# A streaming encoder layer in float32 on one core: the first block's order, S5 output by quarters, and other places for the later mixers

## The reference, cut to what matters

```python
h = rmsnorm(x, norm_mix); z = h @ w_in                 # 1024 x 1536: xl, gl, us of 512 each
xc, new_conv = causal_conv(xl, conv_buf, conv_w, conv_b)      # 4 taps
r, ig = sigmoid(xc @ wa + ba), sigmoid(xc @ wx + bx)          # 8 heads of 64
a = exp(-8 * r * softplus(-lam)); b = sqrt(1 - a*a) * (ig * xc)
hl = scan(h[t] = a[t]*h[t-1] + b[t]); y_lru = hl * gelu(gl)
ys = s5(us)      # 32 groups of 16 channels, 64 complex states each, diagonal recurrence
g = gelu(ys); y_ssm = g * sigmoid(g @ w_glu + b_glu)
mix = concat(rmsnorm(y_lru), rmsnorm(y_ssm)); x = x + mix @ w_out
h2 = rmsnorm(x, norm_ffn); x = x + (silu(h2 @ w_gate) * (h2 @ w_up)) @ w_down   # d_ff 2816
y = rmsnorm(x, norm_final)
```

## Time and profile before

| | us |
|---|---|
| median of 3 runs | 2478.4 (2475.61 to 3758.57) |
| profiled execution, its own time | 2483.81 |
| its span, first to last instruction | 2482.0 |
| TensorE busy | 2244.3 (90%), 11746 matmul records |
| VectorE / ScalarE / GpSimd busy | 1549.7 / 1110.4 / 408.3 |
| mean granted TensorE clock | 0.945 |

### The profile page before, as it was taken

How to read it: one execution, slowest core, us unless ns; L and a number is a source line. 1 busy time by engine, 2 the same in 40 slices (tenths; PEclk the granted TensorE clock), 3 DMA queues, 4 the chain that set the end, 5 groups by cost and what they waited for, 6 DMA issues and landing times.

```text
span 2482.0 us, 30507 instructions
## 1 busy us (share of the span) xinstructions
PE 2244.3 (90%) x11746; PEld 2173.5 (88%) x11746; DVE 1549.7 (62%) x2601; ACT 1110.4 (45%) x1481; POOL 408.3 (16%) x483
## 2 busy tenths in 40 slices
PE   4546589999999999998999999899999989999995
PEld 3536489998899999898999999899999989999995
DVE  6465454667666665876567477656667766664544
ACT  3342433465454356546344454544455544433231
POOL 2453111013110110230111024011102311010001
PEclk9775699999999999999999999999999989999998
DMA  4346133355433535453344546333555543343331
GB/s 146 105 124 176 47 121 118 125 152 164 147 101 107 171 107 154 160 164 113 112 136 154 138 130 203 94 119 110 175 140 152 145 128 111 104 145 119 110 123 52
DMA packets 191073, 322.84 MB, mean 130 GB/s; under 512 B 82896, under 2 KB 121104, under 8 KB 190800
## 3 DMA queue, kind: packets, MB, share of 16 engines
q1 hardware_dynamic: 188560, 313.54, 41.8%
q0 software_dynamic: 2368, 7.34, 1.0%
HBM read 296.39 MB, written 26.53 MB: 130 GB/s over the span
## 4 chain that ended last, share of the span: by engine, by line
PE 78%; DVE 4%; SPq 3%; ACT 2%; POOL 2%; issue 2%; DMA 1%; POOLq 0%; DVEq 0%; ACTq 0%
PE acc L787 25%; PE acc L789 24%; PE acc L788 24%; SPq L449 3%; PE acc L863 1%; PE acc L864 1%; DVE rstd L1041 1%; PE acc L873 1%; POOL tmp L511 1%; PE acc L843 1%; DVE w_hl L924 1%; PE acc L853 1%; DMA g_dram<-u 1%; DVE act_hl L924 1%; POOL s5p L536 0%
## 5 line engine op out<-in xcount | busy, mean ns | idle before, releaser
L787 PE MATMUL acc<-act_hl,w_hl 128*128 128x416 f32 x2640 | 951.8, 361 | 59.0 <-DVE act_hl L924 55.3
L789 PE MATMUL acc<-act_hl,w_hl 128*128 128x416 f32 x2640 | 940.6, 356 | 0.0
L788 PE MATMUL acc<-act_hl,w_hl 128*128 128x416 f32 x2640 | 938.1, 355 | 0.0
L924 DVE TENSOR_TENSOR w_hl<-w_raw,w_hl 128x1024 fp32r<-128x1024 f32 x440 | 545.3, 1251 | 115.0 <-ACT w_hl L611 113.4
L787 PEld LDWEIGHTS acc<-act_hl,w_hl 128*128 128x128 f32 x2640 | 507.6, 192 | 77.9 <-issue 54.6
L788 PEld LDWEIGHTS acc<-act_hl,w_hl 128*128 128x128 f32 x2640 | 507.9, 192 | 8.8 <-issue 3.1
L789 PEld LDWEIGHTS acc<-act_hl,w_hl 128*128 128x128 f32 x2640 | 506.4, 192 | 1.8
L611 ACT ACTIVATE w_hl<-w_raw 128x1024 fp32r<-128x1024 f32 x440 | 454.8, 1051 | 91.0 <-DMA w_raw<-in_w_ffn 45.7
L924 DVE TENSOR_TENSOR x_acc<-x_acc,acc 128x416 f32<-128x416 f32 x480 | 272.5, 585 | 228.6 <-PE acc L789 222.9
L511 POOL TENSOR_TENSOR tmp<-tmp 128x416 f32<-128x416 f32 x135 | 169.7, 1257 | 1193.2 <-ACT tmp L619 1184.6
L787 PE MATMUL acc<-ff_hl,w_hl 128*128 128x416 f32 x880 | 315.1, 358 | 24.8 <-DVE x_acc L924 22.0
(11 more groups left out here) (157 smaller groups left out, 1815.6 us busy)
## 6 DMA issues: line engine op xcount, KB each, us to landing
w_raw<-in_w_ffn SPq DMA_DIRECT2D x330, 512.0 KB, 3.7
w_raw<-in_w_in SPq DMA_DIRECT2D x60, 512.0 KB, 3.5
w_raw<-in_w_out SPq DMA_DIRECT2D x40, 512.0 KB, 3.3
s5y<-y_dram SPq DMA_DIRECT2D x80, 256.0 KB, 4.2
...
```

The costliest lines, as they stand in the source:

```text
L787: pe.matmul(out, w(0), x(0), start=first, stop=False)
L788: pe.matmul(out, w(0), x(1), start=False, stop=False)
L789: return pe.matmul(out, w(1), x(0), start=False, stop=last)
L924: return v.tensor_tensor(out, x, y, op)
```

## The change

1. FIRST is rewritten. The steps are smaller: tb is cut into tb (GpSimd's eight operations), ts (ScalarE's sines) and tr (GpSimd's last operation and its stores); w0 is one unit per step; pb's ScalarE part becomes pq and stands before n1; the VectorE part of xl becomes cv and that of ga becomes bx; the z store becomes zst; c1's store moves into ck. The table steps stand between the products of us, gl and xl, with gl ahead of xl. The LRU steps (la to ld, and xl, cv, ga, bx of tiles 2 and 3) stand between the steps of S5. x comes in two halves, and two units of weights ahead of the parameters.
2. c1t and bmt have two buffers each, tq0 a place of its own, zero lies in kj1 (so ck(1) waits for zero_st). The S5 token buffers begin 6656 bytes further up.
3. The S5 output goes by quarters: gst(j) stores quarter j in 8 DMAs, gld(j) loads it with one, gs(j) splits it. g_dram has another layout.
4. MIXER, the order of all later mixers, is rewritten with the same small steps. Its last step stands at place 60 instead of 64.

The diff, cut to its core:

```diff
+FIRST = [("x", 0), ("pa", 0), ("sq1", 0), ("w0", 0), ("sq1", 1), ("w0", 1), ("sq1", 2), ("w0", 2), ("sq1", 3), ("tb", 0),
+         ("pq", 0), ("n1", 0), ("h1", 0), ("h1", 1), ("h1", 2), ("h1", 3),
+         ("us", 0), ("ts", 0), ("tr", 0), ("tb", 1), ("pb", 0), ("us", 1), ("pc", 0), ("us", 2), ("c1", 0), ("us", 3),
+         ("ts", 1), ("tr", 1), ("tb", 2), ("zst", 0), ("c1", 1), ("gl", 0), ("ck", 0), ("c1", 2), ("gl", 1), ("ck", 1), ("c1", 3),
+         ("gl", 2), ("ck", 2), ("bm", 0), ("ts", 2), ("tr", 2), ("tb", 3), ("gl", 3), ("ck", 3), ("bm", 1), ("bt", 0),
+         ("xl", 0), ("bm", 2), ("bt", 1), ("kt", 0), ("cv", 0), ("bm", 3), ("bt", 2), ("xl", 1), ("ts", 3), ("tr", 3), ("bt", 3),
+         ("zl", 0), ("pl", 0), ("ga", 0), ("bx", 0), ("cv", 1), ("ga", 1), ("bx", 1), ("s5", 0), ("la", 0), ("s5", 1), ("lb", 0),
+         ("s5", 2), ("lc", 0), ("s5", 3), ("ld", 0), ("s5", 4), ("ld", 1), ("xl", 2), ("s5", 5), ("cv", 2), ("s5", 6), ("xl", 3),
+         ("ga", 2), ("s5", 7), ("bx", 2), ("cv", 3), ("gst", 0), ("s5", 8), ("ga", 3), ("bx", 3), ("s5", 9), ("la", 1), ("gld", 0),
+         ("s5", 10), ("lb", 1), ("gst", 1), ("s5", 11), ("lc", 1), ("s5", 12), ("gs", 0), ("ld", 2), ("s5", 13), ("ld", 3),
+         ("gld", 1), ("s5", 14), ("gst", 2), ("s5", 15), ("gs", 1), ("nls", 0), ("s5", 16), ("gld", 2), ("s5", 17), ("gst", 3),
+         ("nls", 1), ("nl", 0), ("gs", 2), ("gld", 3), ("ml", 0), ("ml", 1), ("gs", 3), ("glu", 0), ("glu", 1), ("ns", 0),
+         ("ms", 0), ("ms", 1)] + [("out", d) for d in range(KD)] + [("sq2", 0), ("n2", 0)] + [("h2", i) for i in range(4)]
...
-        LOW = top[0]
+        LOW = top[0] = top[0] + 6656
...
-        zero = sb("zero", [HG, GE, 7 * HG])
+        KJ1 = top[0] + GE * 8 * HG * 4
         kj = [sb(f"kj{i}", [HG, GE, 8, HG]) for i in range(2)]
-        c1t, bmt, rt = [sb(n, [P, GE, 9, HG]) for n in ("c1t", "bmt", "rt")]
-
-        tq = [at("tq0", [P, GE, W5], F32, BB3)] + [sb(f"tq{i}", [P, GE, W5]) for i in (1, 2)]
+        zero = at("zero", [HG, GE, 7 * HG], F32, KJ1)
+        c1t, bmt = [[sb(f"{n}{i}", [P, GE, 9, HG]) for i in range(2)] for n in ("c1t", "bmt")]
+        rt = sb("rt", [P, GE, 9, HG])
+
+        tq = [sb(f"tq{i}", [P, GE, W5]) for i in range(3)]
...
-            load_x(0)
+            for h in range(2):
+                sp.dma_start(x_acc[0][:, 4 * h:4 * h + 4, :], a["x"][0][:, 4 * h:4 * h + 4, 0:T]).then_inc(x_half[h], 16)
+            for u in range(2):
+                load_unit(u)
             for dst, name in ((bc[:], "bc"), (ident[:], "ident"), (dsk[:], "dsk")):
                 sp.dma_start(dst, a[name]).then_inc(par_b, 16)
             sp.dma_start(jrow[:], a["jrow"][:, 0:W5]).then_inc(par_b, 16)
             sp.dma_start(lmask[:], a["lmask"][:, 0:W5]).then_inc(par_b, 16)
-            for u in range(3):
+            for u in range(2, RING):
...
+                elif kind == "zst":
+                    for e in range(KL):
+                        wait_evacuated(sp, ("us", b, e))
                     if b >= 2:
                         sp.wait_ge(u_in, 16 * L * (b - 1))
                     sp.dma_start(z_dram[b % 2].rearrange("e g h s c -> (g h) e (s c)"),
                                  zs[:].rearrange("p e s c -> p e (s c)")).then_inc(z_st, 16)
+                elif kind == "gst":
+                    wait_evacuated(sp, ("y5", b, 4 * j + 1))
+                    wait_evacuated(sp, ("y5", b, 4 * j + 2))
+                    wait_evacuated(sp, ("y5", b, 4 * j + 3))
+                    if b >= 2:
+                        sp.wait_ge(ys_in[j], 16 * (b - 1))
+                    for s in range(L):
+                        sp.dma_start(g_dram[b % 2][j, :, :, s, :].rearrange("g h c -> h g c"),
+                                     u5[s * HG:(s + 1) * HG, j * GE:(j + 1) * GE, :]).then_inc(g_st[j], 16)
+                elif kind == "gld":
+                    sp.wait_ge(z_st, 16 * (b + 1))
+                    sp.wait_ge(g_st[j], 16 * L * (b + 1))
+                    sp.dma_start(zs[:, j].rearrange("p s c -> p (s c)"), g_dram[b % 2][j].rearrange("g h s c -> (g h) (s c)"))\
+                      .then_inc(ys_in[j], 16)
...
+                elif kind == "tr":
+                    g = slice(j * GE, (j + 1) * GE)
+                    po.wait_ge(rho_done, 1)
...
-                elif kind == "c1":
+                elif kind == "ck":
+
                     po.wait_ge(c1_done, j + 1)
-                    po.dma_start(y_dram[:, j * GE:(j + 1) * GE, 0:P], c1t[:, :, 1:9, :].rearrange("p g t h -> p g (t h)"))\
-                      .then_inc(c1_st, 16)
-                elif kind == "ck":
+                    po.dma_start(y_dram[:, j * GE:(j + 1) * GE, 0:P], c1t[j % 2][:, :, 1:9, :].rearrange("p g t h -> p g (t h)"))\
+                      .then_inc(c1_st[j % 2], 16)
...
+                    act.wait_ge(ys_in[j], 16 * (b + 1))
                     if j == 0:
-                        act.wait_ge(ys_in, 16 * G * (b + 1))
                         wait_m(act, ("xl", b, KL - 1))
-                    for n in (2 * j, 2 * j + 1):
-                        act.activation(tokens(act_hl[b % 2][:, 0, KL + n, :]), natural(zs[:, n]), ACT.Copy).then_inc(g_hi, 1)
+                        wait_m(act, ("gl", b, KL - 1))
+                    act.activation(tokens(act_hl[b % 2][:, 0, KL + j, :]), natural(zs[:, j]), ACT.Copy).then_inc(g_hi, 1)
...
+                    if j >= 2:
+                        v.wait_ge(c1_st[j % 2], 16 * (j // 2))
+                        v.wait_ge(ck_prod, 2 * (j - 1))
                     if j:
-                        v.wait_ge(c1_st, 16 * j)
-                        v.wait_ge(ck_prod, 2 * j)
+                        v.wait_ge(c1_done, j)
+                    table(j, 9, c1t[j % 2], bb[:, 2], 0, bc[:, 3], 1, 8, SUB).then_inc(c1_done, 1)
+                elif kind == "bm":
+                    if j >= 2:
+                        v.wait_ge(bt_prod, 2 * (j - 1))
+                    if j:
                         v.wait_ge(bm_done, j)
-                    table(j, 9, c1t, bb[:, 2], 0, bc[:, 3], 1, 8, SUB).then_inc(c1_done, 1)
-                elif kind == "bm":
-                    if j:
-                        v.wait_ge(bt_prod, 2 * j)
-                    v.wait_ge(c1_done, j + 1)
-                    table(j, 8, bmt, bb[:, 0], 0, bb[:, 1], 2, 0, ADD).then_inc(bm_done, 1)
+                    else:
+                        v.wait_ge(c1_done, KL)
+                    table(j, 8, bmt[j % 2], bb[:, 0], 0, bb[:, 1], 2, 0, ADD).then_inc(bm_done, 1)
...
-                elif kind == "xl":
+                elif kind == "cv":
                     if (b, j) == (0, 0):
                         v.wait_ge(par_c, 64)
                     if j >= 2:
                         v.wait_ge(ylru_done, b * KL + j - 1)
-                    wait_evacuated(v, step)
+                    wait_evacuated(v, ("xl", b, j))
...
-                elif kind == "ga":
-                    wait_evacuated(v, (*step, 1))
+                elif kind == "bx":
+                    wait_evacuated(v, ("ga", b, j, 1))
...
```

More of the change, by code:

```diff
@@ L219, in build @@
         bb = sb("bb", [P, 4, G, HG])
-        BB3 = top[0] - G * HG * 4
         pw = sb("pw", [P, 3, G, NPOW])
@@ L264, in build @@
         dt_done, ang_done, pow_done, pl_done = sem("dt_done"), sem("ang_done"), sem("pow_done"), sem("pl_done")
-        c1_done, c1_st, ck_prod, kj_free, kj_done = sem("c1_done"), sem("c1_st"), sem("ck_prod"), sem("kj_free"), sem("kj_done")
+        c1_done, ck_prod, kj_free, kj_done = sem("c1_done"), sem("ck_prod"), sem("kj_free"), sem("kj_done")
+        c1_st = [sem(f"c1_st{i}") for i in range(2)]
         k_st, zero_st, kt_st = [sem(f"k_st{i}") for i in range(2)], sem("zero_st"), sem("kt_st")
@@ L270, in build @@
         t_st, tau_done, bb_done = [sem(f"t_st{i}") for i in range(3)], sem("tau_done"), sem("bb_done")
+        x_half = [sem(f"x_half{i}") for i in range(2)]
         x_in = [sem(f"x_in{i}") for i in range(2)]
@@ L285, in build @@
         w_done, p_made, x_made, p_done = sem("w_done"), sem("p_made"), sem("x_made"), sem("p_done")
-        g_st, ys_in, g_hi, g_lo, yssm_done = sem("g_st"), sem("ys_in"), sem("g_hi"), sem("g_lo"), sem("yssm_done")
+        g_st, ys_in = [sem(f"g_st{e}") for e in range(KL)], [sem(f"ys_in{e}") for e in range(KL)]
+        g_hi, g_lo, yssm_done = sem("g_hi"), sem("g_lo"), sem("yssm_done")
         nrm, nrm_hi, nrm_lo = sem("nrm"), sem("nrm_hi"), sem("nrm_lo")
@@ L651, in _ @@
                 elif kind == "w0":
-                    for u in range(LEAD_HI):
-                        weight_hi(u)
+                    weight_hi(j)
                 elif kind == "ck":
+                    if j == 1:
+                        act.wait_ge(zero_st, 16 * KL)
                     if j >= 2:
@@ L827, in _ @@
                             ins = pe.matmul(acc[0:HG, bank, (g % 4) * P:(g % 4 + 1) * P], bb[:, 0, j * GE + g, :],
```

(17 more changed lines are left out.)

63 lines of the change are left out of this document (19 added, 44 removed), and 25 rows, old and new, of tables (FIRST, MIXER).

## The result

| | before | after | forecast |
|---|---|---|---|
| median of the runs | 2478.4 us (2475.6 to 2481.4) | 2576.2 us (2573.6 to 2582.2) | 2506 (2425 to 2552) |
| ratio, 95% interval | 1 | 1.0397 [1.0375, 1.0419] | |
| profiled execution, span | 2482.0 | 2571.8 | |
| gate(0) of block 0 starts | 346.75 | 310.26 | 291 |
| S5 of the first block starts | 195 | 154.3 | 133 |

One execution of before, at 3758.6 us, lies half as high again as the three others and is left out. The kernel is slower by 4.0%, outside the range of the forecast. The first block gained 36 us where 56 were forecast, and everything behind gate(0) lost 126 where 84 were forecast.

A forecast was written before the change was run, and what follows sets the result against it. No engine bounds the first block, whose chain saves in full; TensorE is busy 438 of 452 us in later blocks. 2483.8 - 56 (first block) + 84 (four later blocks) = 2512, as a median 2506, range 2425 to 2552.

The forecast's parts named there:

- S5 start: First block, table preparation: S5 starts at 133 instead of 195, -62 us; 150 if GpSimd and VectorE slow each other.
- S5 phase: First block, S5 tokens: 60 us now, 75 with the moved-in VectorE and TensorE work, +15.
- At 2 each, five gaps (e and f are one) cost 10, now 5: Later blocks: half clock behind TensorE's gaps costs 2 us per gap, 10 a block instead of 5.
- (b): Later blocks, ga(3) at place 39 right behind dn: last add, bx(2) and cv(3) make TensorE wait 4.0 us.
- (c): Later blocks, la(1) at place 40 between the gate and the evacuations of y5: TensorE waits 5.2 us.
- (a): Later blocks, ga(1) at place 29: bx(0) and cv(1) stand ahead on VectorE, TensorE waits 4.0 us.
- (d): Later blocks, S5 output by quarters: glu moves to place 52, TensorE waits 5.1 us, as now: even.
- (e): Later blocks, ns directly behind glu(1): TensorE waits 3.9 us, as measured in the first block.
- (f): Later blocks, ms and out share place 54, one gate behind ns: TensorE waits 5.8 us in all.
- R2: Rival: the forecast's gaps at 4 us of clock each, first block gaining only 45: 2557 us; chance 0.12.
- R3: Rival: the forecast's gaps plus gst's issues holding up weight loads, shown by waits for w_hl: 2534 us; chance 0.1.
- landed 48; tb1 57: First block, GpSimd's table chain: tr0's stores land at 48, 3.6 us behind, then tb1 takes 8.7 us, until 57.

The follow-up runs named there:

- e4: The kernel after with its tail alone (glu, ns, ms, out, n2, h2) put back to its old places, gs staying where after has it: 2496.0 us.
- e8: After's first block, the old order of the later mixers up to the S5 output, and after's tail alone left new: 2491.9 us.

## Why the prediction was wrong

The direction of each part was right, and so was the finding that the new order in the later blocks outweighs the first block. Three terms were off, 20 us in the first block and 43 behind it, and they make the 62 us between the forecast for the profiled execution (2512) and its own time (2573.6).

| step | forecast | measured |
|---|---|---|
| S5 start | -62 | -41 |
| S5 phase | +15 | +12 |
| output's way and what follows to gate(0) | -9 | -8 |
| TensorE idle, later blocks | +63 (four times 29.7 - 14) | +78 |
| TensorE slower by its clock, later blocks | +20 (four times 10 - 5) | +49 |

**"At 2 each, five gaps (e and f are one) cost 10, now 5" is the step that failed most.** The count of the gaps was wrong, and their price somewhat low. In the pitch from 1022 to 1506 the granted clock drops to the half at eight places: (b), (c), the S5 stretch from 1102 to 1109 (waits of 0.4 and 0.8 with small matmuls between), glu, ns, out, the wait for w_hl, and (a) of the next block. Over all four later blocks, in us of TensorE's time lost, by the same sum as in the section on the result:

| place | after | forecast for after | before |
|---|---|---|---|
| (a), (b), (c) | 12 times, 27.2 | 24 | none |
| glu, (d) | 4 times, 9.5 | 8 | 4 times, 14.8 |
| ns and out, (e) and (f) | 8 times, 22.7 | 8 | none |
| w_hl behind h2 | 4 times, 10.2 | none | none |
| S5 stretch | 3 times, 8.5 | none | 4 times, 10.3 |
| smaller wait for w_hl; x_acc ahead of n2 | once, 1.7 | none | 3 times, 5.1 |
| sum | 32 times, 80 | 40 | 11 times, 30 (forecast 20) |

So a place costs 2.5, not 2, and there are 32 and not 20 of them. Of the 29 us that the clock took beyond the forecast, 15 come from ns and out: what I took as one is two, 12 us apart, and each pays. 10 come from the wait for w_hl, which was in no list of mine, and 5 from the price of the others. The S5 stretch wasn't in my list either, but before has it too; it makes up for before's 30, which stood in before's trace and which I put at 20. The end of the range for clock, "4 of clock for each gap", would have covered the sum, and R2 gave 2557; but that its 124 us for the later blocks are near the measured 126 is luck, for it was told as 4 us for each of the forecast's gaps, where it was 2.5 for more gaps and longer waits.

**A wait for w_hl behind h2 was not in the sum**, 3.6 us in each block, 14 of the 15 us of idle time beyond the forecast; its clock is in the table. I asked of each moved step what stands in front of the next product of the mixer, and of h2 at place 60 only that "the end at place 60 gives nothing by itself". But a step at place 60 also stands in front of the weight split of the FFN's dn. R3 forecast that very wait, by another mechanism (gst holding up the loads); e4, in which it goes while gst stays where it is, and e8, in which it stays while three of the four gst stand elsewhere, show that it hangs on h2's place, and the timeline shows it behind h2 on VectorE. So R3's trace sign was fulfilled and its reason false, which only a run could tell.

**First block: "landed 48; tb1 57" is the step that failed**, by 4 and then 11 us, and it goes on down the chain. The stores land 5.2 us behind the last issue where I took 3.6, a median over stores with a quieter queue (three landings, some 5 us in all), and tb beside VectorE takes 16.4 and 13.5 instead of 8.7 (12.5 in all); ts(0) came 2 us later. tb(3) ends at 124.9 instead of 107, which is 18 of the 21 missing; the other 3 are SyncE's, whose loads of u took 9.95 instead of 7.1. I had the row that shows the stretching and put it into the bound of 150, not into the value: S5 started at 154.3. The wait of c1(2) came where it was forecast, but with 24.9 instead of 18.

Of the exclusive lock, the Trainium skill says (SBUF — State Buffer, "Who interferes with whom") that a VectorE instruction with two SBUF inputs contends with a GpSimd instruction that reads SBUF, and that the ports they share are an exclusive lock. The trace lies between: tb(1) alone is 8.7 us of GpSimd, the six table operations and three splits beside it 11.8 us of VectorE at their undisturbed 1.36 and 1.22; excluded they would need 20.5, free 11.8, and took 16.4. The 150 of the prediction was nearer than the 133 of the sum. It was worked out from the earlier trace rows, 4 us for each tb, and not from the rule; here tb(1) and tb(3) cost 7.7 and 4.8 more and the two others next to nothing, 12.5 in all instead of 16.

What held: (a) to (f) with their waits, the two waits of 4.0 to within 0.1 in three of four blocks; glu's gap, 4.4 in each block, still there though the 32 loads are gone (before's were 5.1 to 6.5, so it gained some 1.5 a block where even was forecast); the S5 phase; the x halves, which brought nothing (the norm's sum on GpSimd ended at 21.6 instead of 20.4).
